# A ten-item queue for the sample group's attention, with half of the key tiles copied out of PSUM by VectorE

## The chip, the core and the metric

The kernel runs on one core of a Trainium2 chip. The metric is the device time of one execution, in microseconds (us). The kernel before took 2920.98 us, the median of three runs (2914.64 to 2922.89).

## What is computed

One inference step of a two-layer decoder trunk for a prompt of 1024 tokens and a sample group of 8 sequences with one new token each, in float32. Layer 0 is a gated linear recurrence beside a sparse attention of three branches; layer 1 is a gated MLP over chunks; each is followed by a squared-ReLU MLP. The change touches only the attention of the eight samples in layer 0, and of it two branches:

```python
def ab_sample(h, page_table, cache_cmp, cache_sel, win_buf, ...):
    full_sel = jnp.concatenate([gather_pages(cache_sel, page_table), kv_sel], axis=1)    # 2048 old rows + 1
    o_cmp, o_sel = nsa_cmp_sel(q, full_cmp, full_sel, q_pos, pe, w1, w2)                 # 16 of 33 blocks of 64 rows
    kv_w = jnp.concatenate([win_buf, kv_win], axis=1)                                    # the last 512 rows
    o_win = window_attn_dense(q, kv_w, q_pos, k_pos)
```

For both branches the scores are softmax(q K^T), then the product with V. The selected branch scores all 2048 rows of a sample and masks the blocks that were not chosen; the window branch needs 512 rows of each sample.

## The kernel before

The program of each engine (TensorE `pe`, ScalarE `act`, VectorE `dve`, GpSimd `pool`, and SyncE `sp`, which only issues DMAs) is written out by hand. Each engine runs its instructions in the order written, and they wait for one another through semaphores. The sample stage is `sp_sample`, `pool_sample`, `pe_sample`, `act_sample` and `dve_sample`. It stands between the prompt's attention (`pe_nsa`) and the output projection (`pe_about`), and nothing else runs on TensorE in it. PE_S, ACT_S and DVE_S number the steps of an engine, and a wait names the step.

The work comes in ten groups of the same size: eight selected items, one per sample, and two window items of four samples each. For each, TensorE transposes four key tiles (four 128x128 transposes each, L2386 or L2333) into PSUM banks 4 and 5 in turn, ScalarE copies each tile to SBUF (`ktb`, L2504 or L2493), TensorE makes the scores (L2398 or L2339), VectorE masks them and takes the maximum (L2570, L2575), ScalarE makes the exponential (L2508), TensorE transposes the probabilities back (L2406), VectorE copies them (L2585, or L2555 for the window), and TensorE multiplies with the values (L2414 or L2357).

The window groups come first: all eight samples' key tiles, then both softmaxes and products, laced with the first selected item. Each selected item b then goes through one turn of a loop: four key tiles of b (K), the probabilities of b-1 (PT), the scores of b (S), the values of b-1 (V). `other_branches` (L2422 to L2429) adds the compressed and window branches to the output after item 2. After item 7 there is a tail that joins the parts of the softmax (L2596 to L2625).

What sets when data come:

- `window_rows(x)` loads the window rows of two samples into `wrow[x]`, 1.05 MB (128 partitions, 8 pieces of 1 KB each), issued by SP. `new_rows(x)` then waits for that load and adds one new row per sample, 2 KB, on the same queue. There are four `wrow` buffers. Load 0 is made long before the stage; 1 and 2 are issued when the prompt's last scores are done, and 3 after new_rows(2), which had to wait for load 2.
- `gather` loads the selected rows of one sample, 2.1 MB, with four indirect DMAs from GpSimd (L1129), each with rows of 4 KB. There are four `srows` buffers. Gathers 0 to 2 come early; gather 3 waits for the window values (`wv1`); gather b from 4 on waits for the values of item b-4.
- The weights of the projection are loaded and split by GpSimd (`pool_split`, L237 and L240) after the values of item 5.

Of the kernel before, what the change touches and what calls it, by code (L numbers as in the profile page):

```python
# [17 lines left out]
ALU = mybir.AluOpType  # L18
# [23 lines left out]
def build(nc, x_prompt, x_sample, cache_cmp, cache_sel, state_win, state_hgrn, page_table,  # L42
# [5 lines left out]
    with ctx:  # L48
# [2029 lines left out]
        ktb = [at("ktb0", R_W, [P, 4, 512]), at("ktb1", R_G + 24832, [P, 4, 512])]  # L2078
        sc = at("sc", R_H, [P, 2, 512])
        qe = at("qe", R_H + 4096, [R, 16, 64])  # L2080
        wsc = at("wsc", R_H + 4096, [P, 2, 512])
# [34 lines left out]
        ptw = at("ptw", R_H + 27552, [P, 2, 4, P])  # L2116
        osb = at("osb", R_H + 31648, [P, R])
# [11 lines left out]
        def pe_selected():  # L2129
            order = ["K0_0", "K0_1", "wpt0", "K0_2", "wpt1", "K0_3", "wv0", "wv1", "S0"]  # L2130
            for b in range(1, NB):
                order += [f"K{b}_{i}" for i in range(4)] + [f"PT{b - 1}", f"S{b}", f"V{b - 1}"]
                order += ["base"] if b == 2 else []
            return order + ["PT7", "ST", "V7"]

        def act_selected():
            order = ["k0_0", "k0_1", "wx1", "k0_2", "k0_3"]
            for b in range(1, NB):
                order += [f"k{b}_0", f"k{b}_1", f"ex{b - 1}", f"k{b}_2", f"k{b}_3"]
            return order + ["ex7"]  # L2140

        def dve_selected():
            order = ["ma0", "mx0"]
            for b in range(1, NB):
                order += [f"pts{b - 1}", f"ma{b}", f"mx{b}"]
                order += ["osel0"] if b == 5 else []
            return order + ["st", "pts7"]

        PE_S = steps("wk0", "wk1", "pre", "wk2", "wk3", "ws0", "wk4", "wk5", "wk6", "wk7", "ws1",
                     *pe_selected(), "wc", "out", "shift")  # L2150
        ACT_S = steps("cmp", "wk0", "wk1", "wk2", "wk3", "wk4", "wk5", "wx0", "wk6", "wk7",
                      *act_selected(), "rowexp", "hi")
        DVE_S = steps("gg", "pgz", "masks", "qe", "cmpmax", "pcs", "pgsel", "cmpw", "knz", "pre", "wm0", "wm1",
                      "ptw0", "ptw1", "ww", "ow", *dve_selected(),
                      "rowd", "osel1", "wrow", "wsel", "pnT", "osb", "lo")
# [7 lines left out]
        def sp_sample(sp):  # L2163
            def window_rows(x):
                sp.dma_start(wrow[x][:, :, :, :].rearrange("p b i c -> p (b i) c"),
                             state_win[0, 2 * x:2 * x + 2].rearrange("b (i p) a g d -> p (b i) (a g d)", p=P))\
                    .then_inc(s_wr[x], 16)

            def new_rows(x):
                sp.wait_ge(s_wr[x], 16)  # L2170
                sp.dma_start(wrow[x][0:1, :, 0, :], kvs[SEQ + 2 * x:SEQ + 2 * x + 2, 512:768].unsqueeze(0))\
                    .then_inc(s_wr[x], 16)
# [151 lines left out]
        def pe_sample(pe):  # L2324
# [3 lines left out]
            def window_keys(b):  # L2328
                pe.wait_ge(s_wr[b // 2], 32)
                if b >= 2:  # L2330
                    pe.wait_ge(sA, ACT_S[f"wk{b - 2}"])
                for i in range(4):
                    last = pe.transpose(psum[:, 4 + b % 2, i * P:(i + 1) * P], wrow[b // 2][:, b % 2, i, 0:P], ident[:, :])  # L2333
                done(last)

            def window_scores(half):
                pe.wait_ge(sA, ACT_S[f"wk{4 * half + 3}"])
                for j in range(4):
                    last = pe.matmul(psum[32 * j:32 * j + 32, half, :], qm[:, 4 * half + j, 32 * half:32 * half + 32],  # L2339
                                     ktb[half][:, j, :], start=True, stop=True)  # L2340
                done(last)

            def window_probs_back(half):
                pe.wait_ge(sA, ACT_S[f"wx{half}"])
                pe.wait_ge(sD, DVE_S["pre"])
                for i in range(4):
                    last = pe.transpose(psum[:, 2 + half, i * P:(i + 1) * P], wsc[:, half, i * P:(i + 1) * P], ident[:, :])
                done(last)

            def window_values(half):  # L2350
                pe.wait_ge(sD, DVE_S[f"ptw{half}"])
                if half == 0:
                    pe.wait_ge(p_cb, GROUPS)
                for i in range(4):
                    for j in range(4):
                        b = 4 * half + j
                        last = pe.matmul(psum[32 * j:32 * j + 32, 7, P * half:P * half + P],  # L2357
                                         ptw[:, half, i, 32 * j:32 * j + 32], wrow[b // 2][:, b % 2, i, P:2 * P],
                                         start=(i == 0), stop=(i == 3))
                done(last)  # L2360

# [16 lines left out]
            def keys_back(b, i):  # L2378
                if i == 0:
                    pe.wait_ge(s_sr[b % 4], 64 * (b // 4 + 1))  # L2380
                if i >= 2:
                    pe.wait_ge(sA, ACT_S[f"k{b}_{i - 2}"])
                else:
                    pe.wait_ge(sA, ACT_S[f"k{b - 1}_{i + 2}" if b else f"wk{6 + i}"])
                for e in range(4):
                    last = pe.transpose(psum[:, 4 + i % 2, e * P:(e + 1) * P],  # L2386
                                        srows[b % 4][:, i, 256 * e:256 * e + P], ident[:, :])
                done(last)

            def selected_scores(b):  # L2390
                pe.wait_ge(sA, ACT_S[f"k{b}_3"])
                if b >= 2:
                    pe.wait_ge(sD, DVE_S[f"ma{b - 2}"])
                else:
                    pe.wait_ge(sA, ACT_S[f"wx{b}"])
                half = b // 4
                for i in range(4):
                    last = pe.matmul(psum[32 * i:32 * i + 32, b % 2, :], qm[:, b, 32 * half:32 * half + 32],  # L2398
                                     ktb[b % 2][:, i, :], start=True, stop=True)
                done(last)  # L2400

            def probs_back(b):
                pe.wait_ge(sA, ACT_S[f"ex{b}"])
                pe.wait_ge(sD, DVE_S[f"pts{b - 1}" if b else "ptw0"])
                for e in range(4):
                    last = pe.transpose(psum[:, 2, e * P:(e + 1) * P], sc[:, b % 2, e * P:(e + 1) * P], ident[:, :])  # L2406
                done(last)

            def selected_values(b):
                pe.wait_ge(sD, DVE_S[f"pts{b}"])  # L2410
                bank = (6, 3)[b // 4]
                for e in range(4):
                    for i in range(4):
                        last = pe.matmul(psum[32 * i:32 * i + 32, bank, 0:P], pts[:, b % 4, e, 32 * i:32 * i + 32],  # L2414
                                         srows[b % 4][:, i, 256 * e + P:256 * e + 2 * P],
                                         start=(b % 4 == 0 and e == 0), stop=(b % 4 == 3 and e == 3),
                                         skip_group_check=True)
# [19 lines left out]
            window_keys(0)  # L2437
            window_keys(1)
            spread()
            window_keys(2)  # L2440
            window_keys(3)
            window_scores(0)
            for b in range(4, NB):
                window_keys(b)
            window_scores(1)
            keys_back(0, 0)
            keys_back(0, 1)
            window_probs_back(0)
            keys_back(0, 2)
            window_probs_back(1)  # L2450
            keys_back(0, 3)
            window_values(0)
            window_values(1)
            selected_scores(0)
            for b in range(1, NB):
                for i in range(4):
                    keys_back(b, i)
                probs_back(b - 1)
                selected_scores(b)
                selected_values(b - 1)  # L2460
                if b == 2:
                    other_branches()
            probs_back(7)
            pe.wait_ge(sD, DVE_S["st"])
            pe.transpose(psum[0:2, 0, 0:P], st4[:, 0, :], ident[:, :])
            pe.matmul(psum[0:2, 0, P:P + 32], ident[0:2, 0:2], nrow[:, 0, :], start=True, stop=True)
# [514 lines left out]
```

## Time and profile before

| what | value |
|---|---|
| median of three runs | 2920.98 us |
| time of the profiled execution | 2925.13 us |
| its span, first to last instruction | 2923.4 us |
| TensorE matmul busy | 2813.5 us, 96% |
| VectorE busy | 1194.3 us, 41% |
| GpSimd busy | 1009.4 us, 35% |
| ScalarE busy | 625.7 us, 21% |
| mean granted TensorE clock | 0.98 |
| sample stage on TensorE | 940.2 to 1023.2 us of the span |

The shares are means over very different stages. TensorE is nearly always busy in the two MLPs, which take most of the span. The sample stage, 83 us, is one of the few in which it waits. In the rows, times are microseconds from the start of the span, PE is a matmul of TensorE, and an arrow in brackets names what ended the idle time before. A granted clock of 1.00 is 2.4 GHz, and 0.50 is 1.2 GHz.

### The profile page before, as it was taken

How to read it: one execution, taken by the hardware profiler on the slowest of the kernel's cores; microseconds unless marked ns; L12 is line 12 of the kernel's file. 1: busy time of each engine (PE TensorE's matmuls, PEld its weight loads, DVE VectorE, ACT ScalarE, POOL GpSimd, SP SyncE). 2: the span in 40 equal slices, each digit the busy share in tenths (PEclk: the TensorE clock that was granted, in tenths of full speed). 3: DMA queues.
4: the chain of work that ended last, by engine and by line, in shares of the span. 5: the costliest groups of instructions: out<-in, count | busy, mean ns of one | idle time of the engine just before them, and what ended most of it. 6: DMA issues, size and time to landing. Idle time of an engine off the chain costs nothing.

```text
span 2923.4 us, 49276 instructions
## 1 busy us (share of the span) xinstructions
PE 2813.5 (96%) x21195; PEld 2679.2 (92%) x21195; DVE 1194.3 (41%) x1244; ACT 625.7 (21%) x1092; POOL 1009.4 (35%) x484
## 2 busy tenths in 40 slices
PE   7999999999898799999999999999999999999998
PEld 7999878886776599999999999999999999999998
DVE  6121274345443315444334444416335434444345
ACT  4100045556564302001110011311111110001102
POOL 6342100000001444444444444533554444444340
PEclk9999999989998899999999999999999999999999
DMA  5112242300103531111111111311211111111111
GB/s 182 45 46 61 92 133 84 104 13 2 74 2 119 185 109 44 44 51 43 44 49 45 48 43 50 123 37 51 89 43 51 44 49 44 44 50 43 50 50 58
DMA packets 204235, 185.46 MB, mean 63 GB/s; under 512 B 8013, under 2 KB 185426, under 8 KB 202362
## 3 DMA queue, kind: packets, MB, share of 16 engines
q1 hardware_dynamic: 193290, 160.28, 17.5%
q0 software_dynamic: 4608, 16.78, 1.6%
q10 hardware_dynamic: 6192, 6.29, 0.8%
q8 instruction: 113, 1.85, 0.3%
q14 instruction: 32, 0.26, 0.0%
HBM read 162.41 MB, written 25.09 MB: 64 GB/s over the span
## 4 chain that ended last, share of the span: by engine, by line
PE 79%; issue 8%; DVE 6%; ACT 2%; POOL 2%; DMA 2%; SPq 0%; another core or an unknown queue 0%; POOLq 0%; DVEq 0%; ACTq 0%
PE psum L266 50%; PE psum L476 6%; PE psum L298 5%; PE psum L1484 4%; PE psum L1890 2%; PE psum L286 2%; PE psum L1864 2%; DVE xlo L338 2%; POOL whl L237 1%; PE psum L1827 1%; PE psum L1468 1%; POOL whl L240 1%; DVE nmax L1993 1%; DMA wrow<-in_state_win_kv 1%; PE psum L313 1%
## 5 line engine op out<-in xcount | busy, mean ns | idle before, releaser
L266 PE MATMUL psum<-xhi,whl 128*128 128x344 f32 x4704 | 874.7, 321 | 1.7 <-ACT vCs L692 0.6
L237 POOL TENSOR_TENSOR whl<-wraw,zeroc 128x1024 fp32r<-128x1024 f32 x186 | 373.2, 2006 | 1154.6 <-PE psum L266 824.7
L266 PEld LDWEIGHTS psum<-xhi,whl 128*128 128x128 f32 x4704 | 765.7, 188 | 2.6 <-issue 1.7
L240 POOL TENSOR_TENSOR whl<-wraw,whl 128x1024 fp32r<-128x1024 f32 x186 | 501.7, 2697 | 14.6
L266 PE MATMUL psum<-xlo,whl 128*128 128x344 f32 x2352 | 500.0, 321 | 0.0
L266 PE MATMUL psum<-ahi,whl 128*128 128x344 f32 x2304 | 427.4, 319 | 0.2
L266 PEld LDWEIGHTS psum<-xlo,whl 128*128 128x128 f32 x2352 | 398.8, 189 | 0.0
L266 PEld LDWEIGHTS psum<-ahi,whl 128*128 128x128 f32 x2304 | 373.0, 188 | 4.4 <-DVE ftmp L558 3.8
L545 DVE CAST ahi<-frel 128x1032 fp32r<-128x1032 f32 x64 | 171.2, 2675 | 475.5 <-ACT frel L522 475.1
L520 ACT ACTIVATE frel<-psum 128x1032 f32<-128x1032 f32 x64 | 66.2, 1034 | 1232.9 <-PE psum L266 1189.9
L558 DVE TENSOR_TENSOR ftmp<-psum,fscale 128x1032 f32<-128x1032 f32 x127 | 156.4, 1231 | 307.6 <-PE psum L266 247.2
L266 PE MATMUL psum<-alo,whl 128*128 128x344 f32 x1152 | 243.9, 320 | 0.0
L298 PE MATMUL psum<-whl,xhi 128*128 128x256 f32 (+1 forms) x1200 | 215.5, 282 | 4.2 <-DVE kvst L975 2.9
L266 PEld LDWEIGHTS psum<-alo,whl 128*128 128x128 f32 x1152 | 192.4, 188 | 0.0
L561 DVE TENSOR_TENSOR hT<-hT,ftmp 128x1032 f32<-128x1032 f32 x127 | 189.9, 1495 | 4.4
L298 PEld LDWEIGHTS psum<-whl,xhi 128*128 128x128 f32 (+1 forms) x1200 | 175.5, 177 | 8.8 <-DVE kvst L975 3.2
L298 PE MATMUL psum<-whl,xlo 128*128 128x256 f32 (+1 forms) x600 | 168.4, 281 | 0.0
L1129 POOL DMA_INDIRECT srows<-in_cache_sel_kv,idx x32 | 30.3, 946 | 353.5 <-PE psum L1802 265.7
L476 PE MATMUL psum<-ahi,whl 128*128 128x344 f32 x768 | 144.3, 320 | 0.0
L1993 DVE TENSOR_REDUCE nmax<-psum 128x1 f32<-128x640 f32 (+7 forms) x108 | 87.3, 808 | 126.5 <-PE psum L1834 112.0
L1484 PE MATMUL psum<-xp,w1c 128*128 128x254 f32 (+1 forms) x576 | 131.4, 371 | 0.9 <-ACT xp L1308 0.9
L476 PEld LDWEIGHTS psum<-ahi,whl 128*128 128x128 f32 x768 | 125.3, 188 | 0.0
(431 smaller groups left out, 3048.9 us busy)
## 6 DMA issues: line engine op xcount, KB each, us to landing
wraw<-in_w_ffn SPq DMA_DIRECT2D x128, 512.0 KB, 3.8
rows<-in_cache_cmp_kv SPq DMA_DIRECT2D x128, 128.0 KB, 2.5
wraw<-in_w_in_ab SPq DMA_DIRECT2D x26, 512.0 KB, 3.8
hT<-h_spill SPq DMA_DIRECT2D x8, 1032.0 KB, 9.3
wraw<-in_w_in_c SPq DMA_DIRECT2D x16, 512.0 KB, 3.8
h_spill<-hT SPq DMA_DIRECT2D x4, 1032.0 KB, 7.9
h_spill<-hT SPq DMA_DIRECT2D x1, 4128.0 KB, 13.1
wrow<-in_state_win_kv SPq DMA_DIRECT2D x4, 1024.0 KB
```

What stands on the lines that cost most here:

```text
L237: pool.tensor_tensor(whl[:, s, 0, :], raw, zeroc[:, 0:1].to_broadcast([P, UNIT]), ALU.add).then_inc(w_hi, 1)
L240: pool.tensor_tensor(whl[:, s, 1, :], raw, whl[:, s, 0, :].bitcast(F32), ALU.subtract).then_inc(w_ready, 1)
L266: last = pe.matmul(psum[:, 3 * bset + c, 0:TC], w, rhs[ah][:, k0 + k, c * TC:(c + 1) * TC], start=(k == 0 and n == 0), stop=(k == kn - 1 a ...
L286: last = pe.matmul(psum[:, 3 * b + c, 0:TC], whl[:, slot + b, wh, k * P:(k + 1) * P], rhs[ah][:, k, c * TC:(c + 1) * TC], start=(k == 0 an ...
L298: last = pe.matmul(psum[0:m, bank, 0:256].rearrange("m (a b) -> m a b", a=2), (xhi, xlo)[ah][:, k, lo:lo + m], w, start=(k == 0 and n == 0 ...
L476: last = pe.matmul(psum[:, 3 * n + c, 0:TC], w, (ahi, alo)[ah][:, k, c * TC:(c + 1) * TC], start=(k == 0 and p == 0), stop=(k == 3 and p = ...
L520: act.activation(thirds(frel[:, j % 2, :]), pset(j % 2), ACT.Relu).then_inc(f_rel, 1)
L545: dve.tensor_copy(ahi[:, j, :], frel[:, j % 2, :]).then_inc(f_hi, 1)
L558: dve.tensor_tensor(thirds(ftmp[:, n % 2, :]), pset(n % 2), thirds(fscale[:, :]), ALU.mult)\
L561: dve.tensor_tensor(hT[:, n, :], hT[:, n, :], ftmp[:, n % 2, :], ALU.add).then_inc(f_h, 1)
L1484: last = pe.matmul(o, w1c[:, k, j, :], xv[:, :, j % 8, s:s + n], start=(j == 0), stop=(j == 15))
L1993: dve.tensor_reduce(nmax[:, k % 4, 0:hn], s_, AX.X, ALU.max, negate=True).then_inc(p_nm, 1)
```

## The change

The ten groups become one queue of ten items, in the order s0, s1, w0, s2, s3, s4, w1, s5, s6, s7 (s is a selected item, w a window item), and all go through the one loop. Key tiles 0 and 2 of an item are still copied by ScalarE, tiles 1 and 3 now by VectorE. There are only two `wrow` buffers, and window loads 2 and 3 are issued after the values of w0. Gather 3 no longer waits for the window values. Gather 4 goes into buffer 1 behind the values of s1, and gather 5 into buffer 0. `other_branches` stands after the scores of place 8, and the weights of the projection are awaited from the values of s4 (place 5), all but the first unit also from `other_branches`. The amount of work on TensorE is the same.

```diff
-        wrow = [at(f"wrow{x}", R_G + 8192 * (x - 1) if x else R_W + 8192, [P, 2, 4, 256]) for x in range(4)]
+        wrow = [at("wrow0", R_W + 8192, [P, 2, 4, 256]), at("wrow1", R_G, [P, 2, 4, 256])]
+        ITEMS = ("s0", "s1", "w0", "s2", "s3", "s4", "w1", "s5", "s6", "s7")
+        LAST = len(ITEMS) - 1
+        BUFFER = (0, 1, 2, 3, 1, 0, 2, 3)
...
             sp.wait_ge(p_qk, len(SOFT))
             window_rows(1)
+            new_rows(1)
+            sp.wait_ge(sP, PE_S[f"V{place('w0')}"])
             window_rows(2)
-            new_rows(1)
+            window_rows(3)
             new_rows(2)
-            sp.wait_ge(p_pv, len(SOFT))
-            window_rows(3)
             new_rows(3)
...
             pool.memset(pts[:, :, :, :], 0.0).then_inc(s_m16, 1)
-            pool.wait_ge(sP, PE_S["wv1"])
             gather(pool, cache_sel[0], srows[3], 3, s_sr[3])
             for b in range(4, NB):
-                pool.wait_ge(sP, PE_S[f"V{b - 4}"])
-                gather(pool, cache_sel[0], srows[b % 4], b, s_sr[b % 4])
+                x = BUFFER[b]
+                pool.wait_ge(sP, PE_S[f"V{place(f's{x}')}"])
+                gather(pool, cache_sel[0], srows[x], b, s_sr[x])
...
+            keys_back(0, 0)
+            keys_back(0, 1)
+            spread()
+            keys_back(0, 2)
+            keys_back(0, 3)
+            scores(0)
+            for p in range(1, LAST + 1):
+                for i in range(4):
+                    keys_back(p, i)
+                probs_back(p - 1)
+                scores(p)
+                if p == 8:
+                    other_branches()
+                values(p - 1)
...
+            for p in range(LAST + 1):
+                keys(p, 0)
+                if p:
+                    exponential(p - 1)
+                keys(p, 2)
+            exponential(LAST)
...
+            for p in range(1, LAST + 1):
+                keys(p, 1)
+                keys(p, 3)
+                probs(p - 1)
...
+                masked_scores(p)
...
-            sp.wait_ge(sP, PE_S["V5"])
+            sp.wait_ge(sP, PE_S[f"V{place('s4')}"])
...
-            pool.wait_ge(sP, PE_S["V5"])
-            pool_split(pool, phases["ab_out"], 8)
+            pool.wait_ge(sP, PE_S[f"V{place('s4')}"])
+            pool_split(pool, phases["ab_out"], 1)
+            pool.wait_ge(sP, PE_S["base"])
+            pool_split(pool, phases["ab_out"] + 1, 7)
```

## Rows read from the trace of the kernel before

**Rows 1.** Busy time, clock and DMA of two stretches of the sample stage:

```profile
core 0: us, PE busy (x) PEld busy (x) DVE busy (x) ACT busy (x) POOL busy (x), PEclk, DMA share, GB/s
940.00:965.00 25.00, 18.19 (x174) 12.58 (x178) 6.20 (x13) 8.29 (x16) 2.68 (x2) 0.59 0.45 163
...
983.00:1008.00 25.00, 21.47 (x255) 13.97 (x257) 7.17 (x14) 11.94 (x26) 7.67 (x9) 0.97 0.75 260
```

**Rows 2.** Chain of work that ended last, 930 to 956: start, duration, what.

```profile
930.05 17.03 DMA wrow<-in_state_win_kv
...
947.72 5.46 DMA wrow<-in_state_win_kv
953.19 1.89 DMA wrow<-kv_scratch
```

**Rows 3.** Timeline of TensorE, one turn of the loop and the next start:

```profile
986.69 1.09 PE L2386 MATMUL psum<-ident,srows 128*128 128x128 f32 x8
988.03 1.14 PE L2386 MATMUL psum<-ident,srows 128*128 128x128 f32 x8 [0.25 <-issue]
...
990.20 1.06 PE L2398 MATMUL psum<-ktb,qm 128*32 128x512 f32 x8 [0.32 <-ACT ktb L2504]
991.08 1.06 PE L2414 MATMUL psum<-srows,pts 128*32 128x128 f32 x32
992.07 1.42 PE L2386 MATMUL psum<-ident,srows 128*128 128x128 f32 x8
```

**Rows 4.** Timelines of ScalarE and VectorE, same turn, and a window item's copy (L2555):

```profile
987.38 1.09 ACT L2504 ACTIVATE ktb<-psum 128x512 f32<-128x512 f32 x2 [2.62 <-PE psum L2386]
988.36 0.72 ACT L2508 ACTIVATE sc<-sc,st 128x512 f32<-128x512 f32 x1
...
961.73 0.69 DVE L2555 COPY ptw<-psum 128x512 f32<-128x512 f32 x1 [1.25 <-PE psum L2347]
...
989.92 0.29 DVE L2585 COPY pts<-psum 128x128 f32<-128x128 f32 x1 [2.55 <-PE psum L2406]
...
992.06 0.69 DVE L2575 TENSOR_REDUCE st<-sc 128x1 f32<-128x512 f32 x1
```

**Rows 5.** Timeline of TensorE, other places of the sample stage:

```profile
948.21 1.93 PE L2339 MATMUL psum<-ktb,qm 128*32 128x512 f32 x8 [0.69 <-ACT ktb L2493]
950.07 1.97 PE L2333 MATMUL psum<-ident,wrow 128*128 128x128 f32 x8
...
966.38 1.09 PE L2386 MATMUL psum<-ident,srows 128*128 128x128 f32 x8
...
977.31 0.43 PE L2422 MATMUL psum<-zeroc,ident 128*128 128x64 f32 x2
...
980.22 1.07 PE L2386 MATMUL psum<-ident,srows 128*128 128x128 f32 x8
...
1007.41 1.06 PE L2398 MATMUL psum<-ktb,qm 128*32 128x512 f32 x8 [0.32 <-ACT ktb L2504]
```

**Rows 6.** Timelines of SP's DMA queue and of GpSimd, sample stage:

```profile
935.58 12.07 SPq L2171 DMA_DIRECT2D wrow<-kv_scratch  x2
...
940.85 1.82 POOL L2214 MEMSET pts<- 128x2048 f32 x1
...
987.06 0.94 POOL L1129 DMA_INDIRECT srows<-in_cache_sel_kv,idx  x1 [3.91 <-PE psum L2414]
...
1010.18 2.35 POOL L240 TENSOR_TENSOR whl<-wraw,whl 128x1024 fp32r<-128x1024 f32 x1
```

**Rows 7.** Busy time by stretch, columns as in Rows 1, while three loads overlap:

```profile
936.00:938.00 2.00, 0.52 (x3) 0.53 (x4) 1.38 (x2) 0.00 (x0) 1.51 (x2) 0.71 1.04 403
```

**Rows 8.** DMA queues, 860 to 1060: packets, MB, share; q0 gathers, q1 SP's loads:

```profile
q0 software_dynamic: 4608, 16.78, 23.7%
q1 hardware_dynamic: 12028, 11.57, 17.8%
```

**Rows 9.** Timeline of VectorE, the tail's first step:

```profile
1010.84 1.71 DVE L2596 TENSOR_TENSOR stx<-st,own 128x16 f32<-128x16 f32 x1 [0.88 <-ACT sc L2508]
```

More of the change, by code:

```diff
@@ L2116, in build, with place, selected, number @@
         ptw = at("ptw", R_H + 27552, [P, 2, 4, P])
+        ITEMS = ("s0", "s1", "w0", "s2", "s3", "s4", "w1", "s5", "s6", "s7")
+        LAST = len(ITEMS) - 1
+        BUFFER = (0, 1, 2, 3, 1, 0, 2, 3)
+        def place(item):
+            return ITEMS.index(item)
+        def selected(p):
+            return ITEMS[p][0] == "s"
+        def number(p):
+            return int(ITEMS[p][1])
+        def keys_tile(p):
+            return ktb[2 if p == 8 else p % 2]
         osb = at("osb", R_H + 31648, [P, R])
@@ L2129, in pe_selected @@
         def pe_selected():
[L2130 to L2134, printed above, removed]
+            order = ["K0_0", "K0_1", "pre", "K0_2", "K0_3", "S0"]
+            for p in range(1, LAST + 1):
+                order += [f"K{p}_{i}" for i in range(4)] + [f"PT{p - 1}", f"S{p}"]
+                order += ["base"] if p == 8 else []
+                order += [f"V{p - 1}"]
@@ L2136, in act_selected @@
+            return order + [f"PT{LAST}", "ST", f"V{LAST}"]
         def act_selected():
[L2137 to L2140, printed above, removed]
+            order = ["k0_0", "k0_2"]
+            for p in range(1, LAST + 1):
+                order += [f"k{p}_0", f"ex{p - 1}", f"k{p}_2"]
+            return order + [f"ex{LAST}"]
         def dve_selected():
-            order = ["ma0", "mx0"]
@@ L2144, in dve_selected @@
[L2144 to L2152, printed above, removed]
@@ L2153, in build @@
-        DVE_S = steps("gg", "pgz", "masks", "qe", "cmpmax", "pcs", "pgsel", "cmpw", "knz", "pre", "wm0", "wm1",
-                      "ptw0", "ptw1", "ww", "ow", *dve_selected(),
-                      "rowd", "osel1", "wrow", "wsel", "pnT", "osb", "lo")
+            order = ["k0_1", "pre", "k0_3", "ma0", "mx0"]
+            for p in range(1, LAST + 1):
+                order += [f"k{p}_1", f"k{p}_3", f"pts{p - 1}"]
+                order += ["ow"] if p == 8 else []
+                order += [f"ma{p}", f"mx{p}"] if selected(p) else [f"mx{p}"]
+                order += ["osel0"] if p == 6 else ["ww"] if p == 7 else []
@@ L2156, in build @@
+            return order + ["st", f"pts{LAST}"]
+        PE_S = steps(*pe_selected(), "wc", "out", "shift")
+        ACT_S = steps("cmp", *act_selected(), "rowexp", "hi")
+        DVE_S = steps("gg", "pgz", "masks", "qe", "cmpmax", "pcs", "pgsel", "cmpw", "knz",
+                      *dve_selected(), "rowd", "osel1", "wrow", "wsel", "pnT", "osb", "lo")
         sP, sA, sD = sem("sample_pe"), sem("sample_act"), sem("sample_dve")
@@ L2326, in done @@
                 last.then_inc(sP, 1)
[L2328 to L2360, printed above, removed]
             def spread():
@@ L2388, in keys_back, with scores @@
                 done(last)
[L2390 to L2396, printed above, removed]
+            def scores(p):
+                keys_moved(p, 2)
+                keys_moved(p, 3)
+                if p >= 2:
+                    if selected(p - 2):
+                        pe.wait_ge(sD, DVE_S[f"ma{p - 2}"])
+                    else:
+                        pe.wait_ge(sA, ACT_S[f"ex{p - 2}"])
+                n = number(p)
+                half = n // 4 if selected(p) else n
@@ L2412, in selected_values @@
                 for e in range(4):
                     for i in range(4):
[L2414 to L2417, printed above, removed]
+                        t = slice(32 * i, 32 * i + 32)
@@ new lines, in values @@
+                        if selected(p):
+                            last = pe.matmul(psum[t, (6, 3)[n // 4], 0:P], pts[:, n % 4, e, t],
+                                             srows[BUFFER[n]][:, i, 256 * e + P:256 * e + 2 * P],
+                                             start=(n % 4 == 0 and e == 0), stop=(n % 4 == 3 and e == 3),
+                                             skip_group_check=True)
+                        else:
+                            b = 4 * n + i
+                            last = pe.matmul(psum[t, 7, P * n:P * n + P], ptw[:, n, e, t],
+                                             wrow[(b // 2) % 2][:, b % 2, e, P:2 * P], start=(e == 0), stop=(e == 3),
+                                             skip_group_check=True)
@@ L2462, in pe_sample @@
                     other_branches()
[L2463 removed]
+                values(p - 1)
+            probs_back(LAST)
             pe.wait_ge(sD, DVE_S["st"])
[L2465 to L2468 removed]
@@ L2520, in act_sample, with keys @@
-            keys(0, 3)
-            for b in range(1, NB):
-                keys(b, 0)
-                keys(b, 1)
-                exponential(b - 1)
-                keys(b, 2)
-                keys(b, 3)
-            exponential(7)
+            def keys(p, i):
+                act.wait_ge(sP, PE_S[f"K{p}_{i}"])
+                if i == 0 and p >= 2:
+                    act.wait_ge(sP, PE_S[f"V{place('w1')}" if p == 8 else f"S{p - 2}"])
+                act.activation(keys_tile(p)[:, i, :], psum[:, 4 + i % 2, :], ACT.Copy).then_inc(sA, 1)
@@ L2546, in dve_sample, with keys @@
             dve_new_key(dve)
+            def keys(p, i):
+                dve.wait_ge(sP, PE_S[f"K{p}_{i}"])
+                if i == 1 and p >= 2:
+                    dve.wait_ge(sP, PE_S[f"V{place('w1')}" if p == 8 else f"S{p - 2}"])
+                step(dve.tensor_copy(keys_tile(p)[:, i, :], psum[:, 5, :]))
+            keys(0, 1)
             dve.wait_ge(sP, PE_S["pre"])
@@ new lines, in probs @@
+            def probs(p):
+                dve.wait_ge(sP, PE_S[f"PT{p}"])
+                n = number(p)
+                back = psum[:, (5 if p == LAST else 2), :]
+                if not selected(p):
+                    step(dve.tensor_copy(ptw[:, n, :, :].rearrange("p i r -> p (i r)"), back))
+                    return
+                if p == 0:
+                    dve.wait_ge(s_m16, 4)
+                if n >= 4:
+                    dve.wait_ge(sP, PE_S[f"V{place(f's{n - 4}')}"])
+                c = slice(8 * (n % 4), 8 * (n % 4) + 8)
+                step(dve.tensor_copy(pts[:, n % 4, :, :].rearrange("p e (i r) -> p e i r", i=4)[:, :, :, c],
+                                     back.rearrange("p (e i r) -> p e i r", e=4, i=4)[:, :, :, c]))
```

212 lines of the change are left out of this document (92 added, 120 removed).

## The prediction

> **What bounds the kernel now.** I read the shares of each engine first: TensorE is busy 96% of the span, so an edit pays only where TensorE waits. The busy time by stretch shows such a place in the sample stage, 940.2 to 1023.2: its first 25 us have 18.2 us of matmul at a mean clock of 0.59, the turns of the loop 21.5 of 25 us at 0.97 [rows 1]. The chain of waits says why the start is slow: two window loads issued together need 17.0 us, the third comes 5.5 us after it is issued, and its new row 1.9 us later [rows 2]. All that time TensorE has small pieces at half clock, and the first tile of selected item 1 starts at 966.38 [rows 5]. After that one turn of the loop sets the pace, 5.38 us from 986.69 to 992.07 [rows 3].
>
> One turn, read off the timelines with its first transpose at 0: first copy on ScalarE 0.69 [rows 3, 4], third tile 1.34, scores 3.51, values 0.88 after that, next turn 0.99 after that. Between tiles and scores the chain is ScalarE: two copies, the exponential, two copies.
>
> **The turn with both engines.** A 128x512 copy out of PSUM costs ScalarE 0.49 when another follows (two in 1.09, each 0.60) and VectorE 0.69 [rows 4]. At 0: tile 0 copied by ScalarE 0.69 to 1.29, so tile 2 starts at 1.34 as now. VectorE's maximum of the item before ends 0.68 after the turn starts (992.06 + 0.69 against 992.07) [rows 3, 4], so it is free for tile 1: 1.18 to 1.87. Tile 3 goes to TensorE at 1.92 and to VectorE at 2.61 to 3.30. Scores at 3.35, next turn 1.87 later [rows 3]: 5.22 us. The exponential (from 1.18) and the 0.29 copy of probabilities (after 3.22) hide: the first ends by 2.0, transposes back start at 2.4, and the values start at 4.23. So moving half the copies saves 0.16 us a turn, about 1 us in all; from ScalarE's queue it takes more, but the chain now goes tile 1, VectorE, tile 3, VectorE. A window item needs the same turn; it lacks the masking step, which is not on the path. Bounds of a turn: 5.38 (nothing saved) and 5.0 (VectorE as quick as ScalarE's 0.60).
>
> **The start.** Selected item 0 has had its data long since, so no load holds the start. Tiles 0 and 1, then `spread`, which still waits for VectorE until 942.7, because VectorE's last step there ends with GpSimd's memset at 942.67 [rows 6]; tiles 2 and 3 at half clock (about 1 us each, eight transposes 1.97 [rows 5]), scores at 947.3, and place 1 at 949.2 (1.86 later [rows 5]). Place 1 begins at half clock; between 5.2 and 8.7 us (all of it at half clock) I take 6.3, because TensorE is nearly without gaps from there, and between 948 and 966 it got from half clock to full with more gaps [rows 5]. Turns then start at 955.5, 960.7, 965.9, 971.2 and 976.4 for places 2 to 6. Selected item 1 starts 17 us earlier than before, but 10.4 us of that is the two window items, which now come inside the loop.
>
> **With no wait for data** the last scores would start so: place 7 at 981.6, place 8 at 986.9, place 9 after 5.22 + 2.91 for `other_branches` (977.31 to 980.22 [rows 5]) + 1.09 for the half clock behind it (980.22 to 986.69 is 6.47 against 5.38 [rows 3, 5]), so at 996.1, its scores at 999.4. Before: 1007.41 [rows 5]. That is 8.0 us gained. The tail is the same chain in other banks.
>
> **The data of w1.** This is where I expect the gain to be lost. Window loads 2 and 3 are issued after the values of w0, at 966.0, not early in the stage. The gather of s4 is issued after the values of s1, at 961.0, and as the wait for s0 is long met, the gather of s5 follows at once, that of s6 at 971.5 and of s7 at 976.7. From 962.6 (1.6 us from a gather's issue to its first bytes, my estimate) the engines have four gathers of 2.1 MB and two window loads of 1.05 MB to move: 10.5 MB. Three overlapping loads ran at 403 GB/s with a DMA share of 1.04 [rows 7], which is full. 10.5 MB at 400 GB/s is 26 us: 989.
>
> Who is last in this heap? SP's packets have a mean of 0.96 KB (11.57 MB in 12028), the gathers' 3.6 KB [rows 8]. In the trace the second of the two early window loads landed at 947.1 (930.05 + 17.03), though the first had landed at 935.58 [rows 2, 6]: 11.5 us for 1.05 MB beside two gathers, against 5.5 us for the third alone. It got some 90 of 400 GB/s and was finished only when the heap was. At 90 GB/s the two loads need 23 us from 968, or the end of the heap; both say 989 to 991. The new row of load 3 follows 1.9 us behind [rows 2], and tiles 2 and 3 of w1 wait for it. The new row of load 2 sits in SP's queue behind load 3, so tiles 0 and 1 are late as well. I take 992 for tile 2 of place 6, against 977.7 without the wait: TensorE stands still for most of 14 us. Behind its wait stand the scores of w1, the values of s4, and with these the weights of the projection, which have time.
>
> The Trainium skill (DMA: Bandwidth & Descriptors, Queues, rings and completion order) states that a DMA engine takes turns between the queues with work, one packet each. By it SP's loads would have 0.96 of every 4.6 KB, an estimate of 84 GB/s, and two loads 25 us. The trace's 11.5 us for one load agrees.
>
> **The sum.** Tile 2 at 992; two tiles at half clock, the copy, scores and values make place 7 start 5.2 us later, 997.2 (a turn has 3.9 left after its tile 2; 1.3 for the clock). Place 8 at 1002.9 (5.22, and 0.5 for the next item), place 9 at 1012.1 (9.2), scores at 1015.5. Against 1007.41: +8.1 us.
>
> The 0.5: VectorE's small step at 1010.84 took 1.71 us and ended with GpSimd's step of 1010.18 to 1012.53 [rows 6, 9]. The window weights (three such small steps, now after the maximum of place 7) can fall onto GpSimd's first split unit, between 0 and 2.3 us. The tail has as many such steps as before and GpSimd is as busy: nothing, give or take 2.
>
> The Trainium skill (GPSIMD Engine Reference, 1. Specifications) says that GpSimd shares its SBUF interfaces with VectorE's instructions of two SBUF inputs; by it the copies out of PSUM that VectorE gains would not be slowed, and the sum stays.
>
> The profiled execution took 2925.1 us, 4.1 above the median; +8 makes it 2933, and the median 2929, which I predict.
>
> **Rivals.**
> 1. The window loads get half of the bytes beside the gathers. For it: the first early load landed 5.5 us after its issue, with a gather begun [rows 2, 6]. Against it: the second. Then 2.1 MB at 200 GB/s from 968 are there at 979, the last new row at 981, and tile 2 waits 3 us: 8.0 - 3.1 = 4.9 us faster, 2916.
> 2. No wait at all. 8 us faster, 2913. It needs 2.1 MB within the two turns between 966 and 976.4 while gathers run; that is 200 GB/s and no new-row latency.
> 3. In between: load 2 passes quickly as load 1 did, load 3 shares. 0 to 4 us slower or even.
> 4. A longer heap: 10.5 MB at 350 GB/s (the loop's 25 us moved 260 in the mean, with gaps [rows 1]) end 4 us later, and the small steps collide: 13 us slower, 2934. A gather's landing then holds place 5 too.
> 5. The move of the copies does nothing, or lengthens the turn, where VectorE's 0.69 against 0.60 counts: 0 to 1.5 us in all, inside the cases.
>
> The side flips at one point: slower than before from a last new row after 984.5 or so (977.7 + 8.0, less the clock), faster below.
>
> **Chances.** Likeliest case (4 to 11 us slower) 0.50; rival 4 (11 to 17) 0.15; rival 3 and even 0.15; rival 1 0.12; rival 2 0.08. 0.3%, about what a measurement of this kernel can tell from no change, is 8.8 us. Over it on the slow side lie two fifths of the likeliest case and all of rival 4: 0.35. On the fast side a part of rival 2 and of anything not thought of: 0.10. Within: 0.55. The range, 2912 to 2938, goes from rival 2 to rival 4 with some spread of the runs.
>
> **What would show it.** Right: in the timeline of TensorE a gap of some 12 us ahead of the first window tiles of place 6, ended by a new row's DMA, at half clock afterwards; GpSimd's five gathers without the long gap before; turns of 5.2 us elsewhere; the stage ending 8 us later. Wrong: window loads that land within 12 us of their issue, or a turn over 5.4 us with VectorE's copies as releaser.

## The result

The changed kernel took 2929.48 us in the median of six runs (2926.80 to 2933.49), the kernel before 2920.27 in six (2914.64 to 2922.89). The ratio is 1.0043, interval 1.0032 to 1.0054: slower, and by more than the 0.3% that counted as no change. The forecast was 2929.0, but its likeliest class was "within 0.3%".

The spans do not show where the time went, because the two profiled executions reach the sample stage at different times: 940.16 before, 932.83 after, with TensorE's program ahead of it unchanged. So everything below is measured inside the stage, from its first transpose (of `srows` or `wrow`) to the first matmul of the output projection (L266). Before that was 940.16 to 1023.17, 83.0 us. After it is 932.83 to 1026.84, 94.0 us: 11.0 us more. The 83.0 us come from one execution only, and a long one: its 2925.13 us lie above every other time of that kernel on record.

Busy time by stretch of the kernel after, columns as in [rows 1]; the first two stretches are the start of the stage and the 25 us behind it, the third the 25 us from shortly after the wait for the window rows, and the last two single out what the DMA engines do:

```profile
932.00:957.00 25.00, 21.35 (x239) 14.93 (x243) 11.50 (x24) 6.86 (x14) 10.78 (x11) 0.80 0.60 229
957.00:982.00 25.00, 9.89 (x144) 6.94 (x135) 7.12 (x12) 3.79 (x8) 11.59 (x13) 0.82 1.00 370
983.00:1008.00 25.00, 20.50 (x201) 14.44 (x199) 11.80 (x19) 5.65 (x12) 5.15 (x3) 0.77 0.24 69
970.00:972.00 2.00, 0.00 (x0) 0.00 (x0) 0.00 (x0) 0.00 (x0) 1.66 (x2) 1.00 1.05 399
946.00:954.00 8.00, 7.01 (x107) 5.27 (x100) 4.18 (x7) 2.87 (x6) 0.99 (x2) 1.00 0.01 2
```

The start is what the queue was meant to make it: 21.4 us of matmul in 25 at a mean granted clock of 0.80, where before it had 18.2 at 0.59 [rows 1]. Then TensorE works 9.9 of 25 us, while the DMA engines are busy all the time at 370 GB/s. From 946 to 954 they had moved 2 GB/s.

TensorE's timeline of the kernel after, around the wait and at the collision near the end, as [rows 3] and [rows 5]; in brackets the idle time before the instruction and what ended it:

```profile
952.34 1.09 PE L2380 MATMUL psum<-ident,srows 128*128 128x128 f32 x8
...
957.57 1.09 PE L2380 MATMUL psum<-ident,srows 128*128 128x128 f32 x8
...
967.42 1.08 PE L2416 MATMUL psum<-srows,pts 128*32 128x128 f32 x32
982.37 1.97 PE L2380 MATMUL psum<-ident,wrow 128*128 128x128 f32 x8 [13.87 <-DMA wrow<-kv_scratch]
985.97 1.97 PE L2380 MATMUL psum<-ident,wrow 128*128 128x128 f32 x8 [1.63 <-DMA wrow<-kv_scratch]
...
991.38 1.09 PE L2380 MATMUL psum<-ident,srows 128*128 128x128 f32 x8
...
996.61 1.09 PE L2380 MATMUL psum<-ident,srows 128*128 128x128 f32 x8
...
1000.59 1.11 PE L2380 MATMUL psum<-ident,srows 128*128 128x128 f32 x4 [1.98 <-DVE ktb L2533]
...
1008.14 3.42 PE L2380 MATMUL psum<-ident,srows 128*128 128x128 f32 x16
...
1012.38 1.07 PE L2395 MATMUL psum<-ktb,qm 128*32 128x512 f32 x8 [0.39 <-issue]
```

A turn is 5.23 us (952.34 to 957.57). The second window item (w1, place 6) then stands 13.87 us and again 1.63 for new rows, and the eight transposes behind it cost 1.97 instead of 1.09, at a granted clock of 0.50.

The DMA queue of SP in the kernel after (start, duration), as [rows 6]. A line with x2 holds two instructions, from the start of the first to the end of the second. Below it stand the first instructions of gathers 4, 5 and 6:

```profile
957.69 1.57 SPq L2179 DMA_DIRECT2D wrow<-in_state_win_kv  x2
974.03 10.64 SPq L2185 DMA_DIRECT2D wrow<-kv_scratch  x2
```

Load 3 and its new row in the chain of work that ended last, as [rows 2]:

```profile
958.44 25.68 DMA wrow<-in_state_win_kv
984.13 1.80 DMA wrow<-kv_scratch
```

Then GpSimd:

```profile
952.70 0.94 POOL L1129 DMA_INDIRECT srows<-in_cache_sel_kv,idx  x1 [11.92 <-PE psum L2416]
...
957.67 0.94 POOL L1129 DMA_INDIRECT srows<-in_cache_sel_kv,idx  x1 [0.30 <-PE psum L2422]
...
963.17 0.93 POOL L1129 DMA_INDIRECT srows<-in_cache_sel_kv,idx  x1 [0.84 <-PE psum L2416]
```

Window loads 2 and 3 are issued at 957.69. The new row that waits for load 2 goes out at 974.03, so load 2 took 16.3 us. Load 3 lands at 984.12, 26.4 us after the first of the two was issued. TensorE's wait does not end with load 2, though: the first two tiles of w1 also need the 2 KB of its new row, which went out at 974.03 and was there only at 982.37, 8.3 us later. Load 3 stands ahead of it in SP's queue; the new row of load 3, with no load ahead of it, took 1.80 us. The order of these two in the queue was not tried; tiles 2 and 3 need load 3 in any case. The gather of s4 began 5 us before them, and that of s5 goes out in the same moment: its own wait is long met, and it only stands behind the four instructions of gather 4 on GpSimd.

### The profile page after: what moved, and what is told of

It is laid out like the page before. It is cut to its first block, busy times and chain, and to the rows that moved or that the text cites. A ratio compares the mean times of both kernels' runs of the same rounds, so it can differ in the third digit from the quotient of the medians.

```text
span 2926.7 us, 49274 instructions
## 1 busy us (share of the span) xinstructions
PE 2808.7 (96%) x21195; PEld 2676.0 (91%) x21195; DVE 1205.6 (41%) x1264; ACT 616.1 (21%) x1072; POOL 1008.8 (34%) x484
## 4 chain that ended last, share of the span: by engine, by line
PE 79%; issue 8%; DVE 7%; POOL 2%; ACT 2%; DMA 2%; SPq 0%; POOLq 0%; DVEq 0%; ACTq 0%
PE psum L266 49%; PE psum L476 6%; PE psum L298 5%; PE psum L1484 4%; PE psum L1890 2%; PE psum L286 2%; DVE xlo L338 2%; PE psum L1864 2%; POOL whl L237 1%; PE psum L1468 1%; PE psum L1827 1%; POOL whl L240 1%; DMA wrow<-in_state_win_kv 1%; DVE nmax L1993 1%; DMA wraw<-in_w_in_ab 1%
## 5 line engine op out<-in xcount | busy, mean ns | idle before, releaser
L266 PE MATMUL psum<-xhi,whl 128*128 128x344 f32 x4704 | 874.1, 320 | 1.7 <-ACT vCs L692 0.6
L266 PEld LDWEIGHTS psum<-xhi,whl 128*128 128x128 f32 x4704 | 765.1, 188 | 2.6 <-issue 1.7
L266 PE MATMUL psum<-xlo,whl 128*128 128x344 f32 x2352 | 499.9, 321 | 0.0
L266 PE MATMUL psum<-ahi,whl 128*128 128x344 f32 x2304 | 427.5, 319 | 0.2
L266 PEld LDWEIGHTS psum<-xlo,whl 128*128 128x128 f32 x2352 | 398.8, 189 | 0.0
L266 PEld LDWEIGHTS psum<-ahi,whl 128*128 128x128 f32 x2304 | 373.1, 188 | 4.4 <-DVE ftmp L558 3.7
L266 PE MATMUL psum<-alo,whl 128*128 128x344 f32 x1152 | 243.9, 320 | 0.0
L266 PEld LDWEIGHTS psum<-alo,whl 128*128 128x128 f32 x1152 | 192.4, 188 | 0.0
```

The lines of the kernel that those rows point to most:

```text
L266: last = pe.matmul(psum[:, 3 * bset + c, 0:TC], w, rhs[ah][:, k0 + k, c * TC:(c + 1) * TC], start=(k == 0 and n == 0), stop=(k == kn - 1 a ...
```

## The experiments

All eight are measured by the stage of one profiled execution and by the time of several runs. A difference of 2 or 3 us between two stages can belong to the two executions and not to the edit, as e7 and e8 below show; the ratios rest on many executions, but their intervals are wide. The column "by the ratio" is the ratio to the kernel before, less one, times its median (2920.27, 2917.56 or 2918.7 us), with its interval:

| kernel | stage, us | against 83.01 | TensorE waits for DMA | median, us | by the ratio, us |
|---|---|---|---|---|---|
| changed kernel | 94.01 | +11.0 | 13.87 + 1.63 + 0.32 | 2929.48 | +12.6 (9.3 to 15.8) |
| e1, gather 5 behind the loads | 80.32 | -2.7 | 0.87, 5.53, 1.50, 0.37 | 2918.44 | +1.5 (-1.5 to 4.4) |
| e2, w1 without loads | 70.45 | -12.6 | none | 2906.96 | -6.4 (-10.8 to -2.3) |
| e3, copies back on ScalarE | 90.03 | +7.0 | 15.03 + 1.06 | 2927.50 | +9.3 (5.3 to 13.1) |
| e4, split behind the base | 90.84 | +7.8 | 15.14 + 0.47 + 0.93 | 2926.27 | +9.9 (5.8 to 13.7) |
| e5, windows at places 0 and 5 | 73.35 | -9.7 | none | 2907.91 | -11.1 (-14.9 to -7.0) |
| e6, 4 KB pieces | 83.43 | +0.4 | 2.64, 3.83, 1.25 | 2919.14 | -0.3 (-3.8 to 3.5) |
| e7, e5 and e6 together | 69.82 | -13.2 | none | 2908.71 | -9.9 (-12.8 to -7.0) |
| e8, before with 4 KB pieces | 78.97 | -4.0 | 3.94, 0.21 | 2916.00 | -3.2 (-5.8 to -0.6) |

### Without the loads

```diff
-            sp.wait_ge(sP, PE_S[f"V{place('w0')}"])
-            window_rows(2)
-            window_rows(3)
-            new_rows(2)
-            new_rows(3)
...
-                    pe.wait_ge(s_wr[b // 2], 32)
+                    if n == 0:
+                        pe.wait_ge(s_wr[b // 2], 32)
```

> The changed kernel without window loads 2 and 3 and their new rows: w1 works on the rows of w0, which leaves out the reading of the last four samples' window rows. Theory S: the whole loss is the wait for these loads: no gap at place 6, stage 75 to 79 us. If something else in the queue of ten were dear (VectorE's copies, the order of the places), the stage would stay above 83 though no load is waited for.

The stage is 70.45 us, shorter than the 75 to 79 expected, and has no wait for data. So the two loads cost 23.6 us of the changed kernel's stage (94.01 - 70.45), more than the 15.8 us of waits in the table: in the rest are the half clock behind the wait and the collision of e4, which e2 does not have (VectorE's step there takes 0.22 us). The queue by itself is worth 12.6 us of stage against the one profile of before. The runs say less than the stage, 6.4 us by the ratio, in an interval 8.5 us wide.

### The order on the DMA engines

```diff
                 pool.wait_ge(sP, PE_S[f"V{place(f's{x}')}"])
+                if b == 5:
+                    pool.wait_ge(s_wr[2], 16)
+                    pool.wait_ge(s_wr[3], 16)
                 gather(pool, cache_sel[0], srows[x], b, s_sr[x])
```

> The changed kernel, but GpSimd issues the gather of s5 (and so those of s6 and s7 behind it) only when window loads 2 and 3 have landed. No byte and no instruction of work is left out. Theory S (the window loads are late because they share the DMA engines with four gathers, a small packet against a large one): the two loads land within 10 us of their issue (first 16.3 us, second about 26 in the changed kernel), the 13.9 us and 1.6 us gaps of TensorE ahead of w1 shrink below 2 us together, the gathers of s5 to s7 are still in time, and the stage (94.0 us in the changed kernel, 83.0 before) falls to 75 to 79, so 2911 to 2917 us in all. Rival B (what counts is the sum of bytes, not their order): the wait moves from w1 to s5, s6 or s7, and the stage stays above 88. Rival W (window loads of 1 KB pieces are slow of themselves beside a running loop): they still take over 14 us each pair half, and the stage stays above 88.

TensorE's timeline of this kernel, the four starts that waited for a DMA, then SP's queue:

```profile
965.41 1.09 PE L2383 MATMUL psum<-ident,srows 128*128 128x128 f32 x8 [0.37 <-DMA srows<-in_cache_sel_kv,idx]
...
972.61 1.09 PE L2383 MATMUL psum<-ident,wrow 128*128 128x128 f32 x8 [0.87 <-DMA wrow<-kv_scratch]
...
982.00 3.83 PE L2383 MATMUL psum<-ident,srows 128*128 128x128 f32 x16 [5.53 <-DMA srows<-in_cache_sel_kv,idx]
990.09 1.09 PE L2383 MATMUL psum<-ident,srows 128*128 128x128 f32 x8 [1.50 <-DMA srows<-in_cache_sel_kv,idx]
```

```profile
959.86 1.67 SPq L2179 DMA_DIRECT2D wrow<-in_state_win_kv  x2
968.11 3.29 SPq L2185 DMA_DIRECT2D wrow<-kv_scratch  x2
```

With only the gather of s4 beside it, load 2 lands 8.3 us after its issue instead of 16.3, load 3 about 3 us later, and w1 waits 0.87. The gather held back is now the late one: it is issued at 971.64, and s5 starts at 982.00 after 5.53 us. So the part of the expectation that no gather would be late was wrong, and the stage is above the 75 to 79 expected. Half of the wait has changed its owner, half (7.6 us) is gone. The stage is shorter by more than that, 13.7 us, among other things because place 8 to place 9 takes 8.0 us instead of 11.5: the collision of e4 is hidden here. The late loads were thus due to the sharing with the gathers, and not to the loads' bytes by themselves.

### The size of the pieces

```diff
-                sp.dma_start(wrow[x % 2][:, :, :, :].rearrange("p b i c -> p (b i) c"),
-                             state_win[0, 2 * x:2 * x + 2].rearrange("b (i p) a g d -> p (b i) (a g d)", p=P))
+                sp.dma_start(wrow[x % 2][:, :, :, :].rearrange("p b i c -> p b (i c)"),
+                             state_win[0, 2 * x:2 * x + 2].rearrange("b (p i) a g d -> p b (i a g d)", p=P))
```

Each partition now reads four adjacent rows, 4 KB at once, instead of four rows of 1 KB that lie apart.

> The changed kernel, but the window rows are laid out so that a partition holds four neighbouring rows, so each load has 256 pieces of 4 KB instead of 1024 of 1 KB; the same bytes, and the softmax does not depend on the order of the rows. Theory S (the DMA engines take turns by packet, so the window loads get 1 KB for 4 KB): with equal packets they get half of the bytes, the pair is complete within 11 to 13 us of its issue instead of 26, the gaps ahead of w1 fall from 15.5 us to 2 to 4, the gathers beside them land later, perhaps 0 to 5 us of waits at s5 to s7, stage 80 to 84. Rival Q (the queue of SP comes second whatever the packets) or B (the sum of bytes): the pair stays above 20 us and the gap above 10.

SP's queue of this kernel, load 3 in the chain that ended last, then the queue's packets, MB and share in the stretch 860 to 1060 (as [rows 8]):

```profile
957.17 1.55 SPq L2179 DMA_DIRECT2D wrow<-in_state_win_kv  x2
966.75 5.49 SPq L2185 DMA_DIRECT2D wrow<-kv_scratch  x2
```

```profile
957.91 13.77 DMA wrow<-in_state_win_kv
```

```profile
q1 hardware_dynamic: 10051, 11.74, 17.7%
```

The loads move the same bytes at the same place in the order, and the queue has 10051 packets in that stretch instead of 12028. Load 2 lands in 9.6 us instead of 16.3, and load 3 lands 14.5 us after the first issue (971.68) instead of 26.4. Nothing else is changed, so the loads' share beside the gathers does depend on the size of their pieces: 2.1 MB in 14.5 us is 145 GB/s, where it was 2.1 in 26.4, 80. Little of this is the larger pieces being quicker by themselves: issued ahead of the gathers, load 2 takes 5.1 us in pieces of 4 KB (e7, 947.21 to 952.31) and 6.1 in pieces of 1 KB (e5). The pair is slower than the 11 to 13 us expected, and the waits ahead of w1 are 6.5 us where 2 to 4 were expected. The stage is 10.6 us shorter. The Trainium skill (DMA: Bandwidth & Descriptors, Queues, rings and completion order) says that an engine drains a packet of one queue before it turns to the next; both numbers go that way. The prediction's estimate of 84 GB/s for 1 KB pieces came near the 80 measured, but the same working gives half of 400 GB/s for 4 KB pieces, and 145 were measured. It also took the profile's packets for those that the Trainium skill means, which no run shows.

> The kernel before with the window rows in 4 KB pieces, nothing else. Before, TensorE waits at the start of the stage for loads 1 to 3 (17.0, then 5.5 and 1.9 us). Theory S: load 2 lands 10 to 13 us after its issue beside two gathers instead of 17.0, load 3 is issued that much earlier but then meets the gathers, and the stage shrinks from 83.0 by 3 to 6 us, time 0.1 to 0.2% lower. Rival B or Q: load 2 lands at 16 to 17 us as before, and the stage stays within 1 us of 83. This run also shows once more how much the start of the stage moves from one execution to the next.

The loads of this kernel in the chain that ended last:

```profile
927.08 10.44 DMA wrow<-in_state_win_kv
938.15 9.09 DMA wrow<-in_state_win_kv
```

With the same edit on the kernel before, the second of its early loads takes 10.4 us, where it took 17.0 [rows 2]. The third follows at once and takes 9.1 us, longer than the 5.5 before, as more goes on beside it. The last new row goes out 20.6 us after the first issue (926.62 to 947.26) instead of 23.6 (929.60 to 953.19): 3.0 us earlier. The stage is 4.0 us shorter, the runs 3.2: in that kernel too a part of the start was the sharing.

Most of the 4.0 us of the stage are something else, though. The stage begins 8.5 us after the first issue here and 10.6 before, so selected item 1 starts only 0.9 us earlier in it. 2.6 us more come from the places behind: four of the five plain turns take 5.35 to 5.38 us here, one 5.65, while the profile of before has turns of 5.56, 6.47, 5.38, 5.70 and 6.14 us, the second with a granted clock of 0.66 from 980 to 985. Nothing shows that the size of the pieces causes these. If they belong to that one execution, the +11.0 us of the changed kernel's stage are some 2 us too few, which would fit the 12.6 by the ratio; this is not shown.

### Another place in the order

```diff
-        ITEMS = ("s0", "s1", "w0", "s2", "s3", "s4", "w1", "s5", "s6", "s7")
+        ITEMS = ("w0", "s0", "s1", "s2", "s3", "w1", "s4", "s5", "s6", "s7")
-        BUFFER = (0, 1, 2, 3, 1, 0, 2, 3)
+        BUFFER = (0, 1, 2, 3, 0, 1, 2, 3)
...
-            pool_split(pool, phases["ab_out"], 1)
-            pool.wait_ge(sP, PE_S["base"])
-            pool_split(pool, phases["ab_out"] + 1, 7)
+            pool.wait_ge(sP, PE_S[f"V{place('s5')}"])
+            pool_split(pool, phases["ab_out"], 8)
```

> The ten items in another order: w0 s0 s1 s2 s3 w1 s4 s5 s6 s7, the four buffers in turn, the weight splits behind the values of s5. Window loads 2 and 3 are issued behind the values of place 0, some 14 us into the stage, when in the changed kernel the DMA engines stand idle, and each gather from s4 on has three turns or more. Theory S (only the place of the loads in time costs): no wait for data over 1 us, stage 70 to 73 us against 83.0 before and 70.5 without the loads, time 0.3 to 0.5% below before. Rival B (10.5 MB have to pass in the middle of the stage whatever their order): waits of 5 us or more at s4 to s7, stage 78 or more, time as before.

SP's queue, the first gather instruction, and w1's first tiles (now place 5) of this kernel:

```profile
947.16 1.12 SPq L2179 DMA_DIRECT2D wrow<-in_state_win_kv  x2
953.25 3.44 SPq L2185 DMA_DIRECT2D wrow<-kv_scratch  x2
```

```profile
952.64 0.94 POOL L1129 DMA_INDIRECT srows<-in_cache_sel_kv,idx  x1 [11.72 <-PE psum L2416]
```

```profile
962.74 1.09 PE L2380 MATMUL psum<-ident,wrow 128*128 128x128 f32 x8
964.17 1.16 PE L2380 MATMUL psum<-ident,wrow 128*128 128x128 f32 x8 [0.34 <-ACT ktb L2490]
```

The loads use the stretch in which the engines were idle in the changed kernel. They are issued 10.5 us earlier, 5.5 us ahead of the first gather; load 2 takes 6.1 us, and w1 begins without a wait. The edit also moves all of GpSimd's weight splits behind the values of s5, so that nothing collides in place 8 (the step for the window weights takes 0.23 us); its gain over the changed kernel is not the loads' alone. The stage of 73.35 us is just above the 70 to 73 expected. The time is 2907.91 us, ratio 0.9962 (0.9949 to 0.9976): this is faster than both kernels, 0.4% below the one before.

> The order of e5 together with the 4 KB pieces of e6. Where e5 has no wait for the window rows left, theory S expects the same stage within 1 us (70 to 73), and 0.3 to 0.5% below before. If window load 1, which meets two gathers ahead of place 0, is late in e5, the larger pieces take that wait away and e7 is shorter by it.

The ratio is 0.9966 (0.9956 to 0.9976), the same as without the larger pieces. Where the loads have the engines nearly to themselves, the size of their pieces is worth nothing that can be seen in the time. The stage of the one profile is 3.5 us shorter, not within 1 us as expected. 2.5 of it lie before the last scores: TensorE had its full clock in places 1 and 9, where it was at half for a while in e5 (place 1 began 7.4 us after the start of the stage against 8.3, place 2 12.7 against 14.1; the clock from 985 to 990 is 1.00 against 0.67). The other 1.0 is in the tail.

### The copies

All four copies of an item back on ScalarE (`keys(p, 0)` to `keys(p, 3)` in `act_sample`, none in `dve_sample`), the queue as it is.

> The changed kernel with all four key tiles of an item copied by ScalarE again, the ten-item queue kept. My reading of the turn: 5.38 instead of 5.22 us, so the stage grows by 1 to 2 us and the wait at w1 stays as long (the loads are issued a little later, 0.3 us). Rival (VectorE's copies are a real gain, or a real loss): the turn changes by over 0.5 us either way, the stage by over 4.

TensorE's first transposes of three places of this kernel:

```profile
954.72 1.09 PE L2377 MATMUL psum<-ident,srows 128*128 128x128 f32 x8
...
960.11 1.09 PE L2377 MATMUL psum<-ident,srows 128*128 128x128 f32 x8
...
965.53 1.09 PE L2377 MATMUL psum<-ident,srows 128*128 128x128 f32 x8
```

A turn is 5.39 to 5.42 us, against 5.23: the copies on VectorE save 0.16 to 0.19 us a turn. It can't be seen in the total. The stage is even 4.0 us shorter here, where 1 to 2 us more were expected. Half of it lies before the last scores, and the next experiment says why; the other half is the tail, where TensorE had its full clock again (the last values take 1.08 us against 1.93).

### The collision

```diff
-            pool_split(pool, phases["ab_out"], 1)
             pool.wait_ge(sP, PE_S["base"])
-            pool_split(pool, phases["ab_out"] + 1, 7)
+            pool_split(pool, phases["ab_out"], 8)
```

> The changed kernel, but GpSimd splits the first weight unit of the projection also after other_branches instead of ahead of it, so that it runs nothing while VectorE makes the window weights after place 7. If VectorE's 2.35 us step there is held up by GpSimd's split, it falls to 0.2 us, TensorE's 1.98 us gap in place 8 closes, and the stage shortens by 2 to 3 us. If the step is slow for another reason it stays at over 1.5 us and the stage within 0.5 us of 94.0. The later unit must not make the projection wait: it is ready some 12 us ahead.

VectorE and GpSimd in the kernel after, then the same step of VectorE in this one:

```profile
997.59 2.35 DVE L2589 TENSOR_TENSOR wwin<-e32w,wst 128x64 f32<-128x64 f32 x1
999.86 0.68 DVE L2533 COPY ktb<-psum 128x512 f32<-128x512 f32 x1
```

```profile
997.51 2.35 POOL L240 TENSOR_TENSOR whl<-wraw,whl 128x1024 fp32r<-128x1024 f32 x1
```

```profile
1000.44 0.22 DVE L2589 TENSOR_TENSOR wwin<-e32w,wst 128x64 f32<-128x64 f32 x1
```

The step for the window weights takes 0.22 us alone and 2.35 beside GpSimd's subtraction, and ends with it. Behind it VectorE's copy of tile 1 is late, which exists only since the copies moved, and TensorE waits 1.98 us. Place 8 to place 9 takes 11.53 us in the kernel after (996.61 to 1008.14) and 8.79 in this one (999.47 to 1008.26): the collision costs 2.7 us, 1.98 of it the wait. In e3 VectorE's step is just as long (2.27 us, L2578 there), but no key copy waits behind it, and place 8 to place 9 takes 9.3 us. The runs can't tell either of them from the changed kernel: their intervals overlap, so the 2.7 us are shown by profiles alone.

## Why the prediction was right or wrong

Times are from the start of the stage in each profile, since the stages begin at different times.

- *The turn.* 5.22 forecast, 5.23 measured.
- *The start.* Place 1 at 9.0 forecast, 8.3 measured; place 2 at 15.3, measured 14.2; the turn at half clock took 5.95 where 6.3 was taken. Right within 1.1 us, a little too dear: `spread` was said to wait for a VectorE step held by GpSimd's memset, but here that step had ended (933.13) before the memset began (934.13), and there was no wait.
- *The data of w1.* Tile 2 of place 6 at 51.8 forecast, 53.1 measured. The shared rate was put at 90 GB/s for the two loads, and was 80 (2.1 MB in 26.4 us). The gathers were issued at 19.9 and 24.8 us (forecast 20.8 and right behind), the DMA engines moved 393 to 397 GB/s from 976 to 982, and load 3 landed as that ended, so the reading of the order was right: the heap and its last items were as described, and so was the new row of load 2 stuck behind load 3.
- *Behind the wait.* Place 7 at +5.2 forecast, +5.4 measured; place 8 at +5.7, measured +5.2.
- *Place 8 to 9: mis-sized.* 9.2 forecast, 11.5 measured. The collision of a small step with a GpSimd unit was seen, but taken as 0.5 us between 0 and 2.3, and counted a place earlier. It struck almost in full. Without it e4 measured 8.8. The scores came 4.2 after place 9 began, 3.4 forecast; that is TensorE at half clock, and not the collision's, as e4 has 4.1.
- *The last scores.* +8.1 forecast. Measured 79.6 us after the start against 67.3 before: +12.3, of which 2.7 is the collision. The terms were off by +1.3 (tile 2, with the start in it), +0.2, -0.5, +2.3 (place 8 to 9) and +0.9.
- *The tail.* "The same, give or take 2": it is 14.5 us against 15.8, which is inside that. The step of [rows 9] is as slow as before, 1.77 us. A later small step (L2611 before, L2607 after) takes 0.18 us instead of 1.52; before, it ended with a GpSimd step of 1016.76 to 1018.65, and now GpSimd runs nothing beside it:

```profile
1017.17 1.52 DVE L2611 TENSOR_TENSOR rows<-rows,nrow 2x32 f32<-2x32 f32 x1
```

```profile
1015.80 1.77 DVE L2592 TENSOR_TENSOR stx<-st,own 128x16 f32<-128x16 f32 x1 [0.88 <-ACT sc L2496]
...
1022.18 0.18 DVE L2607 TENSOR_TENSOR rows<-rows,nrow 2x32 f32<-2x32 f32 x1
```

  So the stage is +11.0, not +8.
- *The total.* The forecast set the +8 against the profiled execution of before, then took off 4.1 for its distance from the median, and came out 0.5 us from the measured median. Part of that is luck: by the ratio the change costs 12.6 us, 9.3 at the lower end of the interval, and the stage 11.0. The sum was 3 us short by the stage, and this does not show in the total, as the medians lie 9.2 us apart. The mechanism was right: the wait at w1, its length and the half clock behind it. The likeliest class, within 0.3% at 0.55, did not come.

Of the rivals, the second (no wait) named the right mechanism for what the queue could give, but e2 shows 12.6 us where it had 8.0: `other_branches` came without half clock behind it (place 8 to 9 is 7.95 us in e2, where 9.2 was put), the start was quicker, and the tail was 2.3 us shorter, with quicker small steps and the last values at full clock. The first (half of the bytes for the loads) is refuted for 1 KB pieces and comes nearer with 4 KB pieces, where the loads had 145 GB/s. The third lies between and did not occur. Of the fourth the collision came, but not the heap longer by 4 us: tile 2 of w1 was 1.3 us later than forecast, and the stage, at +11, lies at the border between it and the likeliest case. The fifth holds for the total, though not for the turn: the copies' 0.2 us a turn is less than one collision that they allow.

So the chance on "slower by over 0.3%" looks too low at 0.35: the collision was priced from one row [rows 9] as rare, though the new order put them a turn apart: the first split unit's weights behind the values of s4 (990.38), the three small steps behind the maximum of place 7 (996.59).

## What to carry to other kernels

When loads move from before a loop into it, write down every transfer that the same few events release, and ask which of them is needed first: here a load needed in two turns was issued with a gather that had three, and the gather won. Move the load to where the engines are idle (e5) rather than hold the others back (e1, which only moved half of the wait). And when an engine takes over work on the critical chain, look at what its small steps wait for: a step that had cost nothing now stands ahead of a copy.

## What the runs showed that had not been expected

- A load of the same bytes at the same place in the order took 16.3 us in pieces of 1 KB and 9.6 us in pieces of 4 KB beside the same gathers, and 6.1 us in pieces of 1 KB when issued ahead of them. How the engines divide their time in detail was not measured.
- A VectorE step of 128x64 with both inputs in SBUF took 2.35 us instead of 0.22 beside a GpSimd step of 2.35 us and ended with it, while its copies out of PSUM beside such steps kept their 0.69:

```profile
1009.06 2.35 POOL L240 TENSOR_TENSOR whl<-wraw,whl 128x1024 fp32r<-128x1024 f32 x1
```

```profile
1010.15 0.69 DVE L2533 COPY ktb<-psum 128x512 f32<-128x512 f32 x1 [4.39 <-PE psum L2380]
```

  The Trainium skill (GPSIMD Engine Reference, 1. Specifications) names VectorE's instructions of two SBUF inputs among those that contend for the shared interfaces; these rows agree.
- The stage of the kernel before began at 940.16, those of all nine later profiles at 932.8 to 935.3, e8 among them, which differs from it only in the pieces of the window loads. Its profiled time was also 4.9 us over its median. What ahead of the stage varies from one execution to the next was left open. It may be a part of why runs of one kernel differ by 8 us and more, and it is why stages were compared here rather than spans.
